# Token halves of 272 and 256 columns, and streamed tiles at multiples of 64 bytes, in a two-block fp32 network

## The chip, the cores and the metric

The kernel runs on one NeuronCore of a Trainium2 chip. The metric is the device time of one execution in microseconds (us); the times below are medians of several. The engines are PE (TensorE; PEld is its load of a stationary tile), DVE (VectorE), ACT (ScalarE), POOL (GpSimd) and SP (SyncE, which issues most DMAs here).

## The reference, cut to what matters

Two networks run one after the other on 512 tokens of width 1,024, all in float32.

```python
def reference(x, c, ctx, ...):
    x = first_block(x, c, ctx, ...)     # "block 1"
    return second_block(x, meta, ...)   # "block 2"

def second_block(x, meta_tokens, ...):
    h = jnp.concatenate([meta, x], axis=1)          # 16 + 512 = 528 tokens
    for i in range(2):
        a = rmsnorm(h, norm_mix_pre[i])
        m = forgetting_attention(a, ...) if i % 2 == 0 else gated_deltanet(a, ...)
        h = h + rmsnorm(m, norm_mix_post[i])
        f = conv_ffn(rmsnorm(h, norm_ffn_pre[i]), ...)
        h = h + rmsnorm(f, norm_ffn_post[i])
    return h[:, 16:]

def conv_ffn(h, w_up, conv_w, w_down):              # 1024 -> 2 * 2816 -> 1024
    gate, up = jnp.split(causal_dwconv(h @ w_up, conv_w), [2816], axis=-1)
    return (jax.nn.gelu(gate, approximate=True) * up) @ w_down
```

Block 1 is a layer with neighbourhood attention, a state-space scan and a feed-forward part (1,024 to 2 x 2,816 and back) on 512 tokens, with 256 context tokens beside them in the first projections. Most of the work of both blocks is dense projections of the form tokens x weight matrix.

## The kernel before

Everything on the chip lies transposed: features on the 128 partitions, tokens along the free dimension. A weight matrix is worked off in panels of 128 output columns. `panels` is the list of all of them in order, each with its stage ("q", "k", "v", "dt", "xbc", "z", "wo", "up1", "down1" in block 1; "gate", "pair", "sig", "ao", "up2", "down2", "rate", "qkv", "og", "do", "up3", "down3" in block 2), the rows it contracts (kc tiles of 128, mostly 8) and its `spans`, the stretches of tokens. Block 1's spans are 512 columns (`ONE`), or 512 and 256 (`TWO`, with the context). Block 2's are `HALF`: its 528 tokens do not fit in one PSUM bank of 512, so they are worked in two stretches, each in a bank of its own.

The products are made in three parts for the precision: a weight panel is cut into a high part `wh` (ACT, line 613) and the rest `wl` (POOL or DVE, line 623), and an activation into a high part and a rest. `tensor_mm` issues, for each panel j and each contraction tile k, high x high, rest x high and high x rest. This is line 645 of the profile, where each matmul has its own load of the stationary weight tile:

```python
wt, a = ((wh, high), (wh, low), (wl, high))[n]
for i, (t0, tn) in enumerate(p.spans):
    ins = pe.matmul(ps[bank_of(j, i)][:, 0:tn], wt[slot][:, k, :], a[:, k, t0:t0 + tn], start=first, stop=last)
```

All these operands are float32r. The moving operands (`high`, `low`) are `t_hh`/`t_hl` in the first projections of both blocks, `t_mh`/`t_ml` before w_out of block 1, `t_fhh`/`t_fhl` and `t_fh`/`t_fl` in block 1's feed-forward part, and in block 2 `t_hh`, `t_hl`, `t_oh`, `t_ol`, `t_ffh`, `t_ffl`, `t_fhh`, `t_fhl`. The profile leaves out the buffer numbers, so that `t_hh` and `t_fhh` stand for tiles of both blocks; the number of columns (512 and 256, or 264) tells them apart. A panel in block 2 is 8 x 3 x 2 = 48 matmuls. There are two slots of `wh` and `wl`: the cut of panel j waits until panel j-2 has been multiplied.

In the up stages of block 2 (88 panels, in pairs of one gate and one value panel, in groups of 8, 8 and 6 pairs for each feed-forward part), DVE takes a panel out of PSUM (line 2562), ACT starts the convolution over tokens (2736), DVE adds two more taps (2829, 2832), ACT makes the gelu (2740), DVE multiplies gate and value (2838), and ACT and POOL cut the result into high part and rest (2745, 2871). Each engine takes its work in the order in which the program lists it; semaphores join them.

Addresses: `sbt` allots the tiles of a stack one behind the other, and each starts at the next multiple of 32 bytes. A row of 528 columns is 2,112 bytes, which is 33 times 64; rows of 512 and 768 are also multiples of 64. So the base of a tile decides for all its rows. Worked out from the sizes: in the kernel before, block 1's `t_hh`, `t_hl`, `t_mh`, `t_ml` and all weight tiles start at a multiple of 64; `t_fhh`, `t_fhl`, `t_fh`, `t_fl`, and all streamed operand tiles of block 2, start at 32 modulo 64. A second half that begins at column 264 begins 1,056 bytes on, 32 modulo 64 from the base, so at a multiple of 64.

Of the kernel before, what the change touches and what calls it, by code (L numbers as in the profile page):

```python
# [19 lines left out]
L = S + NM  # L20
# [4 lines left out]
TILES = [(0, NM)] + [(NM + 128 * i, 128) for i in range(4)]  # L25
HALF = [(0, L // 2), (L // 2, L // 2)]
NEG = -1e30
# [93 lines left out]
def program(nc, io):  # L121
    ctx = ExitStack()
    with ctx:
# [43 lines left out]
        small = sbt(ctx, "small", [128, 48])  # L167
        eps = sbt(ctx, "eps", [128, 1])
        warm = sbt(ctx, "warm", [128, 1])
        part = [sbt(ctx, f"part{i}", [128, 128]) for i in range(3)]  # L170
        ssq = sbt(ctx, "ssq", [128, 6])
        roots = [sbt(ctx, f"roots{i}", [128, 20]) for i in range(4)]
# [3 lines left out]
        rstd = sbt(ctx, "rstd", [128, S + CT + 4])  # L176
        sqb = [sbt(ctx, f"sqb{i}", [128, S + CT + 4]) for i in range(2)]

        def C(name, p=128, w=128):
# [481 lines left out]
        zs = sbt(s1, "zs", [128, 4, S])  # L661
        xbc = sbt(s1, "xbc", [128, 8, NW])
        dts = sbt(s1, "dts", [128, 6, 16])
        qT = sbt(s1, "qT", [128, 4, S])
# [1201 lines left out]
        pT = [sbt(sb_, f"apt{i}", [128, 1360]) for i in range(2)]  # L1866
        inv = sbt(sb_, "ainv", [128, L // 2])
        glog = sbt(sb_, "aglog", [128, L])
# [157 lines left out]
        ASPLIT = [(0, 0, 16), (1, 0, 144), (2, 0, 272), (3, 0, 400), (4, 0, 400), (4, 400, 128)]  # L2026
        BSPLIT = [(0, 0, 264), (0, 264, 264), (1, 128, 400), (2, 256, 272), (3, 384, 144), (4, 512, 16)]
        SIGNALS.update({
# [536 lines left out]
        def forget_vector(dv, w, st):  # L2565
# [84 lines left out]
            def mixing(p, half):  # L2650
                bo, bs_ = bank("mixing", p, half)
                q0, wide = HALF[half]
                w.wait_ge(s.weighed, at("weighed", "mixing", p, half))
                if p + half:
                    w.wait_ge(s.scaled, at("scaled", "mixing", p - 1 + half, 1 - half))
                dv.reciprocal(inv[:, :], ps[bs_][:, 0:wide]).then_inc(up("inverted", "mixing", p, half), 1)
                w.wait_ge(s.inverted, at("inverted", "mixing", p, half))
                dv.tensor_tensor(acc0[:, p, q0:q0 + wide], ps[bo][:, 0:wide], inv[:, :],
                                 MUL).then_inc(up("scaled", "mixing", p, half), 1)
# [1036 lines left out]
```

## Time and profile before

| what | value |
|---|---|
| median of 3 runs | 2,736.95 us (2,735.82 to 2,739.54) |
| span of the profiled execution | 2,732.2 us |
| matmuls recorded | 19,794, one weight load each |
| TensorE busy | 2,546.3 us, 93% of the span |
| DVE, ACT, POOL busy | 1,369.3, 973.2, 985.7 us |
| read from and written to HBM | 73 GB/s over the span |

The profile is of one execution, and its span runs from its first to its last instruction. No time of that execution beside its span was given; the span is 4.7 us below the median of the runs. "Busy" of an engine is the union of its instructions' durations; matmuls overlap each other, so a steady stretch shows TensorE 100% busy whatever its pace, and the pace is read from the starts. A fp32 matmul (not float32r) is recorded as two.

### The profile page before, as it was taken

The page shows a single profiled execution, that of the slowest core. Times are in us where ns is not written, and L with a number is a line of the kernel's source. Part 1 is how long each engine was busy: PE and PEld are TensorE (multiplying, and loading weights), DVE is VectorE, ACT ScalarE, POOL GpSimd, SP SyncE. Part 2 cuts the span into 40 slices and gives each one's busy share as a digit, 9 for nine tenths or more (in the row PEclk, how much of TensorE's full clock was granted, in tenths as well). Part 3 has the DMA queues.
Part 4 walks back from the last instruction along what each step waited for, and adds up shares of the span by engine and source line. Part 5 has one row for each costly group of instructions (what it writes and reads, how often), then busy time and mean ns, then how long its engine had stood idle before and what let it go on. Part 6 is the DMA issues. An engine that isn't in the chain of part 4 may idle for free.

```text
span 2732.2 us, 45723 instructions
## 1 busy us (share of the span) xinstructions
PE 2546.3 (93%) x19794; PEld 2286.5 (84%) x19794; DVE 1369.3 (50%) x2057; ACT 973.2 (36%) x1565; POOL 985.7 (36%) x585
## 2 busy tenths in 40 slices
PE   7989978799999999999999999989998979999997
PEld 5877767678888888887999999988988968999997
DVE  4634455462635354444264554466654534727363
ACT  5234344232323444334433332354332224333232
POOL 1743344544444322222434444500002214445444
PEclk9999999999999999999999999999999988999998
DMA  9432120333332221111222332322111012233221
GB/s 248 121 94 63 53 70 24 92 96 97 93 93 87 68 55 47 40 47 40 78 62 85 89 90 85 87 59 70 40 33 36 17 32 59 85 92 87 87 87 60
DMA packets 379927, 201.33 MB, mean 74 GB/s; under 512 B 6464, under 2 KB 377152, under 8 KB 379728
## 3 DMA queue, kind: packets, MB, share of 16 engines
q1 hardware_dynamic: 379728, 198.42, 25.8%
q8 instruction: 156, 2.56, 0.4%
q14 instruction: 43, 0.35, 0.0%
HBM read 196.30 MB, written 2.10 MB: 73 GB/s over the span
## 4 chain that ended last, share of the span: by engine, by line
PE 57%; DVE 22%; ACT 11%; issue 4%; POOL 4%; DMA 1%; POOLq 0%; ACTq 0%; SPq 0%; DVEq 0%
PE ps L645 40%; DVE t_ffy L2829 7%; ACT t_wh L613 5%; DVE t_ffy L2832 2%; ACT t_ffy L2736 2%; DVE t_atq L2628 2%; POOL t_wl L623 1%; PE ps L2436 1%; DVE t_wl L623 1%; DVE t_ffy L2838 1%; PE ps L3061 1%; PE ps L2409 1%; PE ps L2375 1%; PE ps L3080 1%; PE ps L1090 1%
## 5 line engine op out<-in xcount | busy, mean ns | idle before, releaser
L623 POOL TENSOR_TENSOR t_wl<-t_raw,t_wh 128x1024 fp32r<-128x1024 f32 (+2 forms) x268 | 611.1, 2281 | 1030.1 <-ACT t_wh L613 1030.1
L613 ACT ACTIVATE t_wh<-t_raw 128x1024 fp32r<-128x1024 f32 (+2 forms) x323 | 327.7, 1015 | 605.8 <-PE ps L645 562.4
L645 PE MATMUL ps<-t_hh,t_wh 128*128 128x264 f32 (+2 forms) x2048 | 473.4, 310 | 14.4 <-DVE t_dcq L2562 3.6
L645 PE MATMUL ps<-t_hh,t_wl 128*128 128x264 f32 (+2 forms) x2048 | 449.4, 298 | 8.0 <-POOL t_wl L623 4.3
L645 PE MATMUL ps<-t_hl,t_wh 128*128 128x264 f32 (+2 forms) x2048 | 446.0, 299 | 0.0
L645 PEld LDWEIGHTS ps<-t_hh,t_wh 128*128 128x128 f32 x2048 | 323.7, 192 | 36.5 <-issue 17.6
L645 PEld LDWEIGHTS ps<-t_hh,t_wl 128*128 128x128 f32 x2048 | 324.0, 191 | 24.2 <-POOL t_wl L623 6.9
L645 PEld LDWEIGHTS ps<-t_hl,t_wh 128*128 128x128 f32 x2048 | 322.6, 191 | 9.1 <-issue 1.5
L645 PE MATMUL ps<-t_fhh,t_wh 128*128 128x264 f32 (+1 forms) x1040 | 280.9, 324 | 6.5 <-DVE t_fhl L1753 4.9
L645 PE MATMUL ps<-t_fhh,t_wl 128*128 128x264 f32 (+1 forms) x1040 | 281.5, 325 | 4.6 <-POOL t_wl L623 4.5
L2829 DVE SCALAR_TENSOR_TENSOR t_ffy<-t_ffp,t_vec,t_ffy 128x528 f32<-128x528 f32 x88 | 216.8, 2463 | 130.6 <-ACT t_ffy L2736 130.6
L645 PE MATMUL ps<-t_fhl,t_wh 128*128 128x264 f32 (+1 forms) x1040 | 278.4, 323 | 0.0
L645 PEld LDWEIGHTS ps<-t_fhh,t_wh 128*128 128x128 f32 x1040 | 173.9, 190 | 25.3 <-DVE t_fhl L1753 7.9
L645 PEld LDWEIGHTS ps<-t_fhh,t_wl 128*128 128x128 f32 x1040 | 174.2, 190 | 21.3 <-POOL t_wl L623 5.9
L645 PEld LDWEIGHTS ps<-t_fhl,t_wh 128*128 128x128 f32 x1040 | 173.5, 189 | 17.3 <-issue 0.4
L645 PE MATMUL ps<-t_ffh,t_wl 128*128 128x264 f32 x704 | 144.7, 287 | 8.6 <-POOL t_wl L623 7.8
L645 PE MATMUL ps<-t_ffh,t_wh 128*128 128x264 f32 x704 | 144.7, 287 | 5.2 <-ACT t_wh L613 1.5
L645 PE MATMUL ps<-t_ffl,t_wh 128*128 128x264 f32 x704 | 143.5, 286 | 0.0
L2562 DVE TENSOR_TENSOR t_ffp<-ps,t_rstd 128x264 f32<-128x264 f32 x176 | 67.5, 426 | 112.6 <-PE ps L645 111.6
L645 PEld LDWEIGHTS ps<-t_ffh,t_wl 128*128 128x128 f32 x704 | 109.7, 190 | 11.9 <-POOL t_wl L623 11.9
L623 DVE TENSOR_TENSOR t_wl<-t_raw,t_wh 128x1024 fp32r<-128x1024 f32 x55 | 79.0, 1437 | 79.8 <-ACT t_wh L613 79.8
L645 PEld LDWEIGHTS ps<-t_ffh,t_wh 128*128 128x128 f32 x704 | 109.3, 190 | 6.9 <-ACT t_wh L613 5.0
(558 smaller groups left out, 4351.3 us busy)
## 6 DMA issues: line engine op xcount, KB each, us to landing
t_raw<-in_up SPq DMA_DIRECT2D x44, 512.0 KB, 3.8
t_raw<-in_up2a SPq DMA_DIRECT2D x44, 512.0 KB, 3.9
t_raw<-in_up2b SPq DMA_DIRECT2D x44, 512.0 KB, 3.9
t_raw<-in_attn_in SPq DMA_DIRECT2D x33, 512.0 KB, 4.1
t_raw<-in_dn_in SPq DMA_DIRECT2D x33, 512.0 KB, 4.1
t_raw<-in_ada_w SPq DMA_DIRECT2D x32, 512.0 KB, 4.4
t_raw<-in_w_in SPq DMA_DIRECT2D x25, 512.0 KB, 4.4
t_raw<-in_down SPq DMA_DIRECT2D x16, 512.0 KB, 3.8
```

What stands on the lines that cost most here:

```text
L613: ac.activation(wh[slot_of[j]][:, 0:kc, :], raw[r % NRAW][:, 0:kc, :], ACT.Copy).then_inc(up("wh_cut", "cut", j), 1)
L623: eng.tensor_tensor(wl[slot_of[j]][:, 0:kc, :], raw[r % NRAW][:, 0:kc, :], wh[slot_of[j]][:, 0:kc, :].bitcast(F), SUB).then_inc(up(name, " ...
L645: ins = pe.matmul(ps[bank_of(j, i)][:, 0:tn], wt[slot][:, k, :], a[:, k, t0:t0 + tn], start=first, stop=last)
L1090: ins = pe.matmul(ps[b][:, 0:64], pts[i % 2][:, 128 * k:128 * k + 128], V[:, v, 64 * h:64 * h + 64], start=k == 0, stop=k == 3)
L2375: pe.matmul(ps[b][0:tn, 0:wide], aq[p % 3][64 * e:64 * e + 64, t0:t0 + tn], ak[p % 3][64 * e:64 * e + 64, a:a + wide], start=True, stop=False)
L2409: pe.matmul(ps[b][0:tn, 0:wide], ak[p % 3][64 * e:64 * e + 64, t0:t0 + tn], aq[p % 3][64 * e:64 * e + 64, q0:q0 + wide], start=True, stop= ...
L2436: ins = pe.matmul(ps[b][64 * e:64 * e + 64, lo - q0:lo - q0 + n], lhs, pT[e][0:tn, P_AT[k] + lo - t0:P_AT[k] + lo - t0 + n], start=k == 0, ...
L2562: ins = dv.tensor_tensor(a[part_, t0:t0 + tn], ap[part_, :], rstd[part_, t0:t0 + tn], MUL)
L2628: dv.reciprocal(tq[m][:, :], tq[m][:, :]).then_inc(up("inverted", "pair_norm", p, m), 1)
L2736: ac.activation(y, fp[par][:, 0:L], ACT.Copy, scale=col(f"f{n}c0", f + NF * par)).then_inc(up("copied", kind, n, f), 1)
L2829: dv.scalar_tensor_tensor(out=y, in0=u[:, 1:1 + L], scalar=col(f"f{n}c1", f + NF * par), in1=y, op0=MUL, op1=ADD).then_inc(st.up(), 1)
L2832: dv.scalar_tensor_tensor(out=y, in0=u[:, 2:2 + L], scalar=col(f"f{n}c2", f + NF * par), in1=y, op0=MUL, op1=ADD).then_inc(up("conved", ki ...
```

## The change

`HALF` becomes 272 and 256 columns instead of 264 twice. All places that use it follow: the two matmuls of each tile and part in every panel of block 2, the two instructions that take a panel out of PSUM, the sums over features, and in the attention the split of the weights' first key tile (`BSPLIT`) and of the mixing. The buffer `inv` grows to 272 columns. Three tiles of 1, 1 and 6 columns (`eps`, `warm`, `ssq`) become one of 8 (`few`), so 32 bytes in place of three times 32, and two pads of 32 bytes (`gap0`, `gap1`) are set behind the tiles that stay for the whole program and behind `xbc`.

```diff
-HALF = [(0, L // 2), (L // 2, L // 2)]
+HALF = [(0, 272), (272, 256)]
...
-        eps = sbt(ctx, "eps", [128, 1])
-        warm = sbt(ctx, "warm", [128, 1])
+        few = sbt(ctx, "few", [128, 8])
+        eps, warm, ssq = few[:, 0:1], few[:, 1:2], few[:, 2:8]
         part = [sbt(ctx, f"part{i}", [128, 128]) for i in range(3)]
-        ssq = sbt(ctx, "ssq", [128, 6])
...
         sqb = [sbt(ctx, f"sqb{i}", [128, S + CT + 4]) for i in range(2)]
+        sbt(ctx, "gap0", [128, 8])
...
         xbc = sbt(s1, "xbc", [128, 8, NW])
+        sbt(s1, "gap1", [128, 8])
...
-        inv = sbt(sb_, "ainv", [128, L // 2])
+        inv = sbt(sb_, "ainv", [128, HALF[0][1]])
...
-        BSPLIT = [(0, 0, 264), (0, 264, 264), (1, 128, 400), (2, 256, 272), (3, 384, 144), (4, 512, 16)]
+        BSPLIT = [(0, 0, 272), (0, 272, 256), (1, 128, 400), (2, 256, 272), (3, 384, 144), (4, 512, 16)]
...
-                dv.reciprocal(inv[:, :], ps[bs_][:, 0:wide]).then_inc(up("inverted", "mixing", p, half), 1)
+                dv.reciprocal(inv[:, 0:wide], ps[bs_][:, 0:wide]).then_inc(up("inverted", "mixing", p, half), 1)
```

What it does to the addresses, again worked out from the sizes: `t_fhh`, `t_fhl`, `t_fh`, `t_fl` and the streamed operand tiles of block 2's panels go from 32 to 0 modulo 64, and both halves of block 2 begin at a multiple of 64. Nothing moves for block 1's `t_hh`, `t_hl`, `t_mh`, `t_ml` and the weight tiles. Tiles behind an odd number of 32-byte tiles go the other way: `t_aq`, `t_ak`, `t_av`, `t_atq` and `t_ablk` of the attention from 0 to 32.

The program has 16,867 matmuls before and after, in the same order. TensorE's instructions in the attention, where a piece of the panels meets the mixing product of the first half (line 2436, stationary `t_av` or ones, moving `t_apt`). Before:

```order
L645 MATMUL ps<-t_hl,t_wh 128x264 x2
L645 MATMUL ps<-t_hh,t_wl 128x264 x2
L2436 MATMUL ps<-t_apt,t_av 64x264 x2
L2436 MATMUL ps<-t_apt,t_cst 64x264 x2
L2436 MATMUL ps<-t_apt,t_av 64x136 x2
L2436 MATMUL ps<-t_apt,t_cst 64x136 x2
L2436 MATMUL ps<-t_apt,t_av 64x8 x2
L2436 MATMUL ps<-t_apt,t_cst 64x8 x2
```

And the same place after (the line is 2437 then):

```order
L645 MATMUL ps<-t_hl,t_wh 128x272
L645 MATMUL ps<-t_hl,t_wh 128x256
L645 MATMUL ps<-t_hh,t_wl 128x272
L645 MATMUL ps<-t_hh,t_wl 128x256
L2437 MATMUL ps<-t_apt,t_av 64x272 x2
L2437 MATMUL ps<-t_apt,t_cst 64x272 x2
L2437 MATMUL ps<-t_apt,t_av 64x144 x2
L2437 MATMUL ps<-t_apt,t_cst 64x144 x2
L2437 MATMUL ps<-t_apt,t_av 64x16 x2
L2437 MATMUL ps<-t_apt,t_cst 64x16 x2
```

Nothing changed its place; only the widths did, and what the mixing of the first half gains (8 columns a tile) the second half loses.

DVE's instructions at the same mixing product and the panel taken out beside it (`t_ainv` is the reciprocal of the weights' sum, `t_acc` the mixed values, `t_aq` a panel of queries). Before:

```order
L2642 TENSOR_REDUCE t_amx<-ps 128x1 x10
L2647 TENSOR_TENSOR t_amx<-t_amx 128x2
L2656 RECIPROCAL t_ainv<-ps 128x264
L2658 TENSOR_TENSOR t_acc<-ps,t_ainv 128x264
L2562 TENSOR_TENSOR t_aq<-ps,t_rstd 128x264 x2
```

And after:

```order
L2643 TENSOR_REDUCE t_amx<-ps 128x1 x10
L2648 TENSOR_TENSOR t_amx<-t_amx 128x2
L2657 RECIPROCAL t_ainv<-ps 128x272
L2659 TENSOR_TENSOR t_acc<-ps,t_ainv 128x272
L2563 TENSOR_TENSOR t_aq<-ps,t_rstd 128x272
L2563 TENSOR_TENSOR t_aq<-ps,t_rstd 128x256
```

Again the order is the same, and one instruction has 8 columns more and its partner 8 fewer.

## Rows read from the trace of the kernel before

**Rows 1.** The page: span, busy time by engine.

```profile
span 2732.2 us, 45723 instructions
...
PE 2546.3 (93%) x19794; PEld 2286.5 (84%) x19794; DVE 1369.3 (50%) x2057; ACT 973.2 (36%) x1565; POOL 985.7 (36%) x585
```

**Rows 2.** The chain that ended last, the whole span, by line.

```profile
PE ps L645 40%; DVE t_ffy L2829 7%; ACT t_wh L613 5%; DVE t_ffy L2832 2%; ACT t_ffy L2736 2%; DVE t_atq L2628 2%; POOL t_wl L623 1%; PE ps L2436 1%; DVE t_wl L623 1%; DVE t_ffy L2838 1%; PE ps L3061 1%; PE ps L2409 1%; PE ps L2375 1%; PE ps L3080 1%; PE ps L1090 1%
```

**Rows 3.** The same chain in 515:912, by line.

```profile
by line: PE ps L645 89.1%; DVE t_sqb L1749 1.5%; issue 1.5%; ACT t_fhh L1583 1.5%; POOL t_wl L623 1.2%; DVE t_rstd L553 0.9%; PE ps L489 0.7%; PE ps L476 0.7%; DVE t_gy L1765 0.6%; ACT t_wh L613 0.5%; DVE t_xT L2794 0.5%; PE ps L498 0.4%; P
```

**Rows 4.** The chain in 912:1358, 1358:1800, 1800:2290 and 2290:2732, in this order.

```profile
by line: PE ps L645 36.5%; DVE t_atq L2628 10.1%; PE ps L2436 8.0%; PE ps L2409 5.7%; PE ps L2375 5.4%; DVE t_ainv L2656 3.6%; issue 3.1%; PE ps L2385 2.6%; PE ps L2416 2.6%; ACT t_atq L2496 2.0%; PE ps L2350 2.0%; ACT L2496 1.8%; PE ps L23
...
by line: PE ps L645 38.2%; DVE t_ffy L2829 22.5%; ACT t_wh L613 10.0%; DVE t_ffy L2832 7.1%; ACT t_ffy L2736 5.8%; issue 5.6%; DVE t_ffy L2838 3.3%; POOL t_wl L623 2.6%; PE ps L2772 0.9%; PE ps L476 0.7%; PE ps L489 0.6%; ACT t_hh L2722 0.3
...
by line: PE ps L645 29.8%; PE ps L3061 5.5%; PE ps L3080 4.6%; issue 4.3%; PE ps L3084 3.8%; DVE t_wl L623 3.2%; ACT t_wh L613 3.1%; DVE t_dv L3330 2.9%; PE ps L3016 2.3%; DVE t_dq L3330 2.1%; PE ps L3147 2.0%; DVE t_dk L3330 1.8%; POOL t_w
...
by line: PE ps L645 33.8%; DVE t_ffy L2829 22.4%; ACT t_wh L613 10.0%; DVE t_ffy L2832 7.1%; issue 5.9%; ACT t_ffy L2736 5.8%; DVE t_ffy L2838 3.3%; POOL t_wl L623 2.6%; PE ps L489 1.0%; PE ps L498 1.0%; DVE t_xT L2803 0.9%; PE ps L2784 0.8
```

**Rows 5.** Groups by line and form, engine PE: count | busy us, mean ns | idle.

```profile
L645 PE MATMUL ps<-t_hh,t_wh 128*128 128x264 f32 x1712 | 371.0, 298 | 12.1 <-DVE t_dcq L2562 3.6 <-ACT t_hh L2722 3.5 <-ACT t_wh L613 2.6
...
L645 PE MATMUL ps<-t_ffh,t_wh 128*128 128x264 f32 x704 | 144.7, 287 | 5.2 <-ACT t_wh L613 1.5 <-POOL t_ffl L2871 1.5 <-ACT t_acc L2543 1.1
...
L645 PE MATMUL ps<-t_fhh,t_wh 128*128 128x264 f32 x688 | 141.9, 287 | 1.6 <-DVE t_ffp L2562 1.6
...
L645 PE MATMUL ps<-t_fhh,t_wh 128*128 128x512 f32 x352 | 139.0, 395 | 4.9 <-DVE t_fhl L1753 4.9
...
L645 PE MATMUL ps<-t_fh,t_wh 128*128 128x512 f32 x176 | 69.4, 394 | 0.0
...
L645 PE MATMUL ps<-t_oh,t_wh 128*128 128x264 f32 x256 | 54.3, 293 | 3.6 <-POOL t_ol L3518 2.4 <-POOL t_ol L2693 1.2
```

**Rows 6.** Timeline, PE, block 1's up stage: start us, us, what.

```profile
699.63 0.40 PE L645 MATMUL ps<-t_fhh,t_wl 128*128 128x512 f32 x1
...
702.43 0.40 PE L645 MATMUL ps<-t_fhh,t_wl 128*128 128x512 f32 x1
```

**Rows 7.** Timeline, PE, a panel of w_out in block 1.

```profile
471.00 0.39 PE L645 MATMUL ps<-t_mh,t_wh 128*128 128x512 f32 x1
...
476.22 0.39 PE L645 MATMUL ps<-t_mh,t_wl 128*128 128x512 f32 x1
```

**Rows 8.** Timeline, PE, a block 1 panel of 512 and 256 columns.

```profile
83.45 0.52 PE L645 MATMUL ps<-t_hl,t_wh 128*128 128x512 f32 x2
...
91.08 0.51 PE L645 MATMUL ps<-t_hh,t_wl 128*128 128x512 f32 x2
```

**Rows 9.** The same view inside that panel, one pair.

```profile
86.11 0.28 PE L645 MATMUL ps<-t_hh,t_wl 128*128 128x256 f32 x1
86.23 0.39 PE L645 MATMUL ps<-t_hh,t_wh 128*128 128x512 f32 x1
```

**Rows 10.** Timeline, PE, a block 2 panel, two halves of 264.

```profile
1546.43 0.42 PE L645 MATMUL ps<-t_hh,t_wh 128*128 128x264 f32 x2
...
1552.27 0.42 PE L645 MATMUL ps<-t_hh,t_wh 128*128 128x264 f32 x2
```

**Rows 11.** By stretch, groups 0 and 1 of block 2's first up: PE, PEld, DVE, ACT, POOL.

```profile
1399.50:1459.00 59.50, 59.05 (x477) 57.98 (x477) 42.92 (x46) 22.21 (x30) 29.78 (x16) 1.00 0.31 89
1517.20:1604.60 87.40, 87.40 (x720) 87.35 (x719) 58.68 (x61) 32.31 (x44) 43.40 (x21) 1.00 0.31 90
```

**Rows 12.** Timeline, DVE, two pairs of up panels.

```profile
1542.92 2.38 DVE L2829 SCALAR_TENSOR_TENSOR t_ffy<-t_ffp,t_vec,t_ffy 128x528 f32<-128x528 f32 x1 [1.36 <-ACT t_ffy L2736]
...
1554.95 2.38 DVE L2829 SCALAR_TENSOR_TENSOR t_ffy<-t_ffp,t_vec,t_ffy 128x528 f32<-128x528 f32 x1 [1.61 <-ACT t_ffy L2736]
```

**Rows 13.** The chain in order of time, same stretch: start us, us, what.

```profile
1541.22 1.05 ACT t_wh L613
```

**Rows 14.** Timeline, POOL, same stretch.

```profile
1542.34 2.39 POOL L623 TENSOR_TENSOR t_wl<-t_raw,t_wh 128x1024 fp32r<-128x1024 f32 x1 [3.08 <-ACT t_wh L613]
```

More of the change, by code:

```diff
@@ L2655, in mixing @@
                     w.wait_ge(s.scaled, at("scaled", "mixing", p - 1 + half, 1 - half))
-                dv.reciprocal(inv[:, :], ps[bs_][:, 0:wide]).then_inc(up("inverted", "mixing", p, half), 1)
+                dv.reciprocal(inv[:, 0:wide], ps[bs_][:, 0:wide]).then_inc(up("inverted", "mixing", p, half), 1)
                 w.wait_ge(s.inverted, at("inverted", "mixing", p, half))
-                dv.tensor_tensor(acc0[:, p, q0:q0 + wide], ps[bo][:, 0:wide], inv[:, :],
+                dv.tensor_tensor(acc0[:, p, q0:q0 + wide], ps[bo][:, 0:wide], inv[:, 0:wide],
                                  MUL).then_inc(up("scaled", "mixing", p, half), 1)
```

## The prediction

> **What bounds the kernel now.** I read the page first: of a span of 2,732.2 us TensorE is busy 2,546.3 (93%), and no other engine reaches 51% [rows 1]. That looks as if every ns taken off a matmul came back. The chain that ended last says otherwise: the streamed products of line 645 are 40% of it, and DVE, ACT and POOL stand between them [rows 2]. So I split the chain at the stages. In 515:912, block 1's feed-forward, line 645 is 89.1% [rows 3]. In block 2 it is 36.5, 38.2, 29.8 and 33.8% of four stretches of 446, 442, 490 and 442 us [rows 4]. That is 162.8 + 168.8 + 146.0 + 149.5 = 627 us, of 1,820.
>
> Then I read the pace of the streamed products from start to start in steady stretches, since the busy time of one holds latency that the next one covers (the page has 395 ns for one of 512 columns). The clock is at its upper level there, 1.00 or 2.4 GHz [rows 11], so 512 columns stream in 213.3 ns. Four cases, with the address of the moving operand, modulo 64, from the section on the kernel:
> - 512 columns from a base at 32: 2.80 us for 12, 233.3 ns each [rows 6];
> - 512 columns from a base at 0: 5.22 us for 23, 227.0 each [rows 7];
> - 512 and 256 columns in turn, both from 0: 7.63 us for 22 pairs, 346.8 a pair [rows 8], of which the narrow one is about 117 (0.12 by the two rows) and the wide one 230 [rows 9];
> - 264 twice, from 32 and from 0: 5.84 us for 24 pairs, 243.3 a pair [rows 10].
>
> The first two have the same columns, one matmul for each weight tile, and differ in the base. 6.4 ns is the time in which 2.4 GHz streams 15 columns, and 64 bytes are 16 columns: as if a stretch of 64 bytes that is touched in part cost a whole one. 512 columns from 32 touch 33 stretches, from 0 they touch 32; 227.0 / 32 = 7.09 ns for each.
>
> **The change, part by part.**
>
> *Block 1's operands at a multiple of 64.* t_fhh, t_fhl, t_fh and t_fl move from 32 to 0. They are read by (352 + 176) x 3 = 1,584 matmuls of 512 columns [rows 5]. On the chain are 89.1% of 397 = 353.7 us, or 353.7 / 0.2333 = 1,516 of them [rows 3]. At 6.4 ns each: **9.7 us**. The bounds are nothing (the base is not the reason) and 1,584 x 6.4 = 10.1. I take 9.7, because nothing else separates rows 6 from rows 7.
>
> *Block 2's pair.* Lengths 264 + 264 touch 17 + 17 stretches: the first starts at 32 and ends on a boundary, the second starts on it and ends inside one. 272 + 256 touch 17 + 16. The number of columns is 528 in both. By the price of a stretch the pair is 34 x 7.09 = 241.1 now, and 2.2 less than measured; the 512 and 256 pair is 48 x 7.09 = 340.3, and 6.5 less than measured. So a new pair costs 33 x 7.09 = 234.0 and 2.2 to 6.5 more: 236.2 to 240.5. From the other side, if the excess over pure streaming (346.8 - 320.0 = 26.8) is one for each pair of aligned matmuls and 64 bytes play no part, the new pair is 220.0 + 26.8 = 246.8, 3.5 more than now. I take 239.3, in the upper half of the first interval since it is nearest the pair that also alternates wide and narrow: **4.0 ns less** a pair. Ends: 7.1 less, 3.5 more.
>
> How many pairs pay? All four groups of 264 in rows 5 times 3 make 10,080 matmuls, 5,040 pairs. But 627 us of chain are 627 / 0.2433 = 2,577 pairs. The rest hides behind other work, and the up stages show what. Their panels come in pairs, gate and value. TensorE needs 2 x 5.84 = 11.68 us for two [rows 10]; DVE's line 2829 comes back after 1,554.95 - 1,542.92 = 12.03 [rows 12]. That loop holds no matmul: ACT cuts the weights (1.05) [rows 13], POOL makes the low part (2.39, from 1,542.34 to 1,544.73) [rows 14], DVE's line 2829 takes 2.38 and ends 0.6 after POOL [rows 12], although it reads no more than its neighbours, and ACT takes the next cut only after what DVE feeds it. In group 0 TensorE already keeps the loop's pace, 59.5 us for 477 matmuls or 124.7 each; in group 1 it runs ahead at 87.4 / 720 = 121.4 [rows 11] and waits at the end. A faster pair there only makes that wait longer, and up to 12.03 - 11.68 = 0.35 us per two panels a slower one costs nothing.
>
> 2,577 x 4.0 = 10.3 us. In the attention and the delta rule the chain changes engine every few us, and what runs beside it is close behind; I take a fifth off: **8.2 us**.
>
> *The rest.* DVE's and ACT's evacuations go from 264 + 264 to 272 + 256 columns, the same sum. The mixing products of line 2436 keep their number and their sum of columns; fp32 streams at half the pace, so that a stretch has double the time to arrive. t_aq and t_ak move from 0 to 32, and some 400 fp32 matmuls of the attention stream them; t_dT, t_dY and t_dTT move from 32 to 0, read by more, but short ones. At a full 6.4 ns the first is 2.6 us lost, and the second as much won. I take nothing for both, and keep 3 us each way. Semaphores, waits and queues stay as they are, and the three small tiles in one lie in front of everything.
>
> A page speaks against all of this. The Trainium skill, "TensorE: Matmul & The Clock Gate", section "Back-to-back issue gap", has the gap between two matmuls depend on the columns alone (columns / 2.4 + 2.5 ns), and "SBUF — State Buffer", section "Specifications (TRN2)", has lines of 16 bytes, which a base at 32 meets as well as one at 0. By the first an estimate for 512 columns is 215.8 ns; the trace does not agree, it has 227.0 and 233.3. By both pages of the Trainium skill the change would give nothing, and the sum would be 0 in place of 17.9.
>
> **Sum.** 9.7 + 8.2 = 17.9 us. On the profiled execution that is 2,732.2 - 17.9 = 2,714.3 of span; the median shown, 2,736.95, is 4.7 longer than that span, which I keep: 2,719.0.
>
> **The rivals.**
> - *The stretch is the whole story, and all of it is on the path.* The pair falls to 236.2, 2,577 x 7.1 = 18.3, with 9.7 makes 28.0: **2,709**. For it: 233.3 against 227.0. Against it: the 512 and 256 pair lies 6.5 above that rule. Chance 0.18.
> - *Block 2 gives nothing.* What the 256 wins the 272 gives back. 2,736.95 - 9.7 = **2,727.3**. For it: 528 columns are streamed either way. 0.08.
> - *Aligned pairs carry 26.8 whatever their length.* 2,577 x 3.5 = 9.0 lost against 9.7 won: **2,736**, no change. For it: the measured 346.8. Against it: the 264 pair, with 23.3, would then be better for being misaligned. 0.06.
> - *The base plays no part*, and rows 6 and 7 differ by the stage (other weights, other DMA). Then block 2's price per stretch falls too: **2,737**. Against it: both run without a wait and at one matmul per weight tile. 0.06. (The two pages of the Trainium skill named above end here too.)
> - *Slower: the weight load is laid bare.* A load runs beside each matmul, and TensorE's load row is busy 87.35 of 87.40 us [rows 11]. If a load wants the 121.7 ns that a 264 gives it, the 256 gets no shorter, and the 272 pays the 16.7 (230 - 213.3) that the wide member pays in rows 9: 121.7 + 113.3 + 16.7 = 251.7, 8.4 more. 2,577 x 8.4 = 21.6, less 9.7: **2,749**. It decides from 15.2 / 2,577 = 5.9 ns a pair. Against it: a 256 passes at 117 in rows 9, loads and all. 0.05.
>
> **How the numbers follow.** The forecast, 0.57, spans 2,713 to 2,727: a pair at 236.2 or at 242, and 3 us for the fp32 products. With the first two rivals it is 0.83, and they reach from 2,709 to 2,727.3; the range is 2,707 to 2,731, which leaves out the last three. A measurement of this kernel tells 0.2% (5.5 us) from no change. Faster: 0.57 + 0.18 + 0.08 = 0.83. Same: 0.06 + 0.06 = 0.12. Slower: 0.05.
>
> **What would show it.** In the changed kernel's timeline: 24 matmuls of t_fhh and t_fh in 5.44 us, not 5.60; a block 2 panel (24 pairs) in 5.74 us, not 5.84 (5.67 by the first rival, 5.92 by the third, 6.04 by the last); line 2829 (2830 then) still every 12.03 us, with a longer wait of TensorE at the start of the down stages; line 645's share of the chain smaller in block 1. I am wrong if the 256 stays at 121, or if DVE's loop moves with the new addresses, since I take it for fixed: 1% of it is 44 x 0.12 = 5.3 us.

## The result, and the profile after

The changed kernel took 2,741.3 us (median of 20 runs, 2,738.4 to 2,745.8), the kernel before 2,736.2 (20 runs, 2,733.8 to 2,743.3): a ratio of 1.0016, 95% interval 1.001 to 1.0022. It is 5 us slower, where 18 us faster was forecast; the prediction itself had set 0.2% (5.5 us) as the least that it would call a change. The profiled execution took 2,742.6 us, its span 2,740.1.

The page of the changed kernel, the lines that answer to [rows 1], and the row of the granted clock:

```profile
span 2740.1 us, 45723 instructions
...
PE 2554.2 (93%) x19794; PEld 2296.2 (84%) x19794; DVE 1368.6 (50%) x2057; ACT 972.8 (36%) x1565; POOL 985.3 (36%) x585
...
PEclk9999989999999999999999999999999898999998
```

TensorE is busy 8 us longer for the same instructions; nobody else is. The chain in 515:912, as in [rows 3], still belongs to the streamed products:

```profile
by line: PE ps L645 88.9%; issue 1.5%; DVE t_sqb L1750 1.5%; ACT t_fhh L1584 1.5%; POOL t_wl L623 1.2%; DVE t_rstd L553 0.9%; DVE t_gy L1766 0.6%; ACT t_wh L613 0.5%; PE ps L476 0.5%; PE ps L489 0.4%; POOL t_raw L920 0.3%; POOL t_rstd L553 
```

The timeline of TensorE in the changed kernel, at the places of [rows 6, 7, 10] (start us, us, what; 24 matmuls or 24 pairs lie between the two rows of each couple):

```profile
471.40 0.39 PE L645 MATMUL ps<-t_mh,t_wl 128*128 128x512 f32 x1
...
476.89 0.39 PE L645 MATMUL ps<-t_mh,t_wl 128*128 128x512 f32 x1
...
697.00 0.39 PE L645 MATMUL ps<-t_fhh,t_wl 128*128 128x512 f32 x1
...
702.58 0.40 PE L645 MATMUL ps<-t_fhh,t_wl 128*128 128x512 f32 x1
...
1551.33 0.40 PE L645 MATMUL ps<-t_hh,t_wl 128*128 128x272 f32 x2
...
1557.17 0.29 PE L645 MATMUL ps<-t_hh,t_wl 128*128 128x272 f32 x1
```

- t_fhh, whose base is now a multiple of 64: 5.58 us, where 5.44 was forecast and 5.60 was before. The first steady panels of the stage still take 5.60, and so do the last four; those between take 5.58.
- The block 2 panel with 272 and 256 columns: 5.84 us, as with 264 twice.
- t_mh, whose address did not move: 5.49 us, 5.44 before. Nothing in the prediction's account can make this panel slower. **This row is the loose thread.** What did move there is the other operand: merging three small tiles into one set all weight tiles 64 bytes lower, which left them at a multiple of 64 and which I therefore passed over.

The same happens in the first projections of block 1 (operand t_hh, not moved either). Rows of the changed kernel, 21 pairs of 512 and 256 columns apart:

```profile
84.40 0.51 PE L645 MATMUL ps<-t_hl,t_wh 128*128 128x512 f32 x2
...
91.80 0.52 PE L645 MATMUL ps<-t_hl,t_wh 128*128 128x512 f32 x2
```

7.40 / 21 = 352.4 ns a pair, against 346.8 in [rows 8].

Then I followed the start of the last streamed matmul at some ends of stages through the traces, of each kernel two executions (the second ones are e4 and e8 below). The last two columns give how long the granted clock stood at 0.50 in the stretch up to there:

| end of | before, twice | changed, twice | mean change in the stretch | at 0.50 before, twice | at 0.50 changed, twice |
|---|---|---|---|---|---|
| q, k, v and dt | 162.6, 162.3 | 164.1, 163.3 | +1.2 | 10.2, 10.2 | 13.7, 10.2 |
| w_out | 511.9, 515.0 | 516.5, 515.8 | +1.5 | 30.7, 37.5 | 37.5, 37.5 |
| block 1's feed-forward | 905.7, 908.8 | 909.3, 909.0 | -0.8 | 6.8, 6.8 | 6.8, 6.8 |
| attention (ao) | 1348.8, 1351.3 | 1354.7, 1354.4 | +2.6 | 6.8, 3.4 | 10.2, 10.2 |
| feed-forward (up2, down2) | 1769.0, 1771.5 | 1773.5, 1773.4 | -1.3 | 10.2, 10.2 | 6.8, 6.8 |
| delta rule (do) | 2282.9, 2285.6 | 2292.7, 2292.0 | +4.9 | 54.6, 54.6 | 64.9, 68.3 |
| feed-forward (up3, down3) | 2704.2, 2707.0 | 2712.8, 2712.9 | -0.8 | 13.7, 13.7 | 10.2, 10.2 |

Between two executions of one kernel the first 515 us differ by up to 3 us; from there to the end the difference stays within 0.7 us. As far as two executions tell, what happens behind 515 belongs to the program. Most of it sits in the attention and the delta rule, in steps of 1.5 and 3.3 us at single panels. A stretch at half clock in which TensorE sets the pace loses half its length. By that reckoning the clock makes +2.6, -1.7, +6.0 and -1.7 us of the last four stretches, where +2.6, -1.3, +4.9 and -0.8 were measured: 5.1 of 5.4 us in all. At the largest step, by stretch: busy us and number of instructions of PE, PEld, DVE, ACT, POOL, granted clock, DMA. The kernel before:

```profile
2109.70:2116.50 6.80, 6.80 (x69) 6.21 (x66) 1.86 (x4) 1.72 (x5) 0.00 (x0) 1.00 0.14 41
2116.50:2123.30 6.80, 6.80 (x62) 6.59 (x62) 3.76 (x11) 3.72 (x5) 1.41 (x1) 1.00 0.00 0
```

The changed kernel at the same instructions:

```profile
2114.40:2121.20 6.80, 6.80 (x70) 6.21 (x67) 1.85 (x4) 1.77 (x5) 0.00 (x0) 1.00 0.14 41
2121.20:2128.00 6.80, 6.80 (x36) 6.45 (x35) 1.90 (x6) 3.58 (x5) 0.00 (x0) 0.50 0.00 0
```

The work ahead is the same, TensorE is busy all the time in both, and in one of them the granted clock falls to 0.50 (1.2 GHz): 36 matmuls go through where 62 did. 6.8 us at half speed cost 3.4. It is the 3.3 us step.

The clock works the other way too. What the changed kernel wins in up2 and down2 is a fall that only the kernel before has, in both of its executions (1,484.6 in e4). The kernel before:

```profile
1481.80:1485.20 3.40, 3.40 (x18) 3.40 (x17) 0.00 (x0) 0.00 (x0) 1.54 (x1) 0.50 0.67 186
```

The changed kernel at the same instructions:

```profile
1487.70:1491.10 3.40, 3.40 (x31) 3.40 (x29) 0.00 (x0) 0.00 (x0) 1.56 (x1) 1.00 0.68 187
```

### The profile page after: what moved, and what is told of

It is laid out like the page before. It is cut to its first block, busy times and chain, and to the rows that moved or that the text cites. A ratio compares the mean times of both kernels' runs of the same rounds, so it can differ in the third digit from the quotient of the medians.

```text
span 2740.1 us, 45723 instructions
## 1 busy us (share of the span) xinstructions
PE 2554.2 (93%) x19794; PEld 2296.2 (84%) x19794; DVE 1368.6 (50%) x2057; ACT 972.8 (36%) x1565; POOL 985.3 (36%) x585
## 4 chain that ended last, share of the span: by engine, by line
PE 57%; DVE 22%; ACT 11%; issue 5%; POOL 4%; DMA 1%; POOLq 0%; ACTq 0%; SPq 0%; DVEq 0%
PE ps L645 40%; DVE t_ffy L2830 7%; ACT t_wh L613 5%; DVE t_ffy L2833 2%; ACT t_ffy L2737 2%; DVE t_atq L2629 2%; POOL t_wl L623 1%; PE ps L2437 1%; DVE t_wl L623 1%; DVE t_ffy L2839 1%; PE ps L3062 1%; PE ps L2410 1%; PE ps L2376 1%; PE ps L3081 1%; PE ps L1091 1%
## 5 line engine op out<-in xcount | busy, mean ns | idle before, releaser
L645 PE MATMUL ps<-t_hh,t_wh 128*128 128x256 f32 (+2 forms) x2048 | 474.4, 311 | 14.4 <-DVE t_dcq L2563 3.6
L645 PE MATMUL ps<-t_hh,t_wl 128*128 128x256 f32 (+2 forms) x2048 | 451.8, 300 | 8.4 <-POOL t_wl L623 5.4
L645 PE MATMUL ps<-t_hl,t_wh 128*128 128x256 f32 (+2 forms) x2048 | 447.3, 299 | 0.0
L645 PE MATMUL ps<-t_fhh,t_wh 128*128 128x512 f32 (+2 forms) x1040 | 280.8, 324 | 6.5 <-DVE t_fhl L1754 4.9
L645 PE MATMUL ps<-t_fhh,t_wl 128*128 128x512 f32 (+2 forms) x1040 | 280.6, 324 | 4.7 <-POOL t_wl L623 4.6
L645 PE MATMUL ps<-t_fhl,t_wh 128*128 128x512 f32 (+2 forms) x1040 | 278.3, 323 | 0.0
L645 PE MATMUL ps<-t_ffh,t_wl 128*128 128x272 f32 x704 | 144.9, 287 | 8.3 <-POOL t_wl L623 7.8
L645 PE MATMUL ps<-t_ffh,t_wh 128*128 128x272 f32 x704 | 143.4, 285 | 5.2 <-POOL t_ffl L2872 1.5
L645 PE MATMUL ps<-t_ffl,t_wh 128*128 128x272 f32 x704 | 142.8, 284 | 0.0
L2563 DVE TENSOR_TENSOR t_ffp<-ps,t_rstd 128x272 f32<-128x272 f32 (+1 forms) x176 | 67.5, 425 | 111.1 <-PE ps L645 110.2
```

Of the source, the lines that this page charges most:

```text
L2563: ins = dv.tensor_tensor(a[part_, t0:t0 + tn], ap[part_, :], rstd[part_, t0:t0 + tn], MUL)
```

## The experiments

Two questions came out of this. Does the pace of a streamed product hang on where its moving tile lies, or on where that lies **against the weight tile**? And do the falls of the clock belong to what the changed kernel does, or only to when it does it? "Distance" below is the address of the moving tile less that of the weight tile, modulo 256, worked out from the sizes in the order of allotment. In block 1 it is the same for every contraction tile and every weight slot, since weights advance by 512 bytes from tile to tile and 4,096 from slot to slot, and the moving tile by 2,048. In block 2 the moving tile's rows of 2,112 bytes walk by 64. Before: t_mh 0, t_fhh 96. Changed: t_mh 64, t_fhh 128. In block 2 the third weight slot (for one panel at the start of a stage) is left out. Ratios are to runs of the kernel before made beside each experiment.

### The parts of the change, alone

**e1: only the halves.** The edits to `HALF`, `BSPLIT` and `inv` of the diff, no pads.

> Only the halves become 272 and 256 (the divisor tile of the attention grows by 32 bytes with them); no pads, so the moving operands stay at 32 modulo 64 as before. If a partly touched 64-byte stretch costs 7.09 ns, 272 from 32 touches 18 and 256 from 32 touches 17, 35 in place of 34: the panel goes from 5.84 to about 6.0 us and the time to about 2,736 + 2,577 x 7.1 ns = 2,754. If only the 528 columns count, the panel stays at 5.84 and block 1 at 5.60, and the time is that of before, about 2,736, unless the split itself is what cost the 5 us of the whole change; then about 2,741.

Measured: 2,742.6 us, ratio 1.0019 (1.001 to 1.0028). Its timeline, 24 pairs of a panel apart:

```profile
1553.24 0.41 PE L645 MATMUL ps<-t_hh,t_wl 128*128 128x272 f32 x2
...
1559.11 0.41 PE L645 MATMUL ps<-t_hh,t_wl 128*128 128x272 f32 x2
```

5.87 us, not the 6.0 of the stretch rule, but not the 5.84 of before either: 1.2 ns a pair, up to 3 us over the 2,577 pairs on the chain. Block 1 stands at 5.60. The halves alone cost as much as the whole change.

**e2: only the pads.** The edits to `few`, `gap0`, `gap1`, halves of 264.

> Only the pads: streamed operands at 0 modulo 64, halves 264 and 264 as before. By the 64-byte stretch block 1 gains 9.7 us and the pair touches 17 + 17 stretches as before: about 2,726. If the base plays no part, block 1's panels stay between 5.57 and 5.60 (gain 0 to 1 us): about 2,735 if the 5 us that the whole change lost belong to the split, about 2,741 if they belong to the addresses or to where the clock falls.

Measured: 2,740.3 us, 1.0015 (1.0006 to 1.0024). t_fhh 5.60 at first and 5.58 later, t_mh 5.49, as in the changed kernel. A panel in up2 takes 5.87 here too (median), and the granted clock falls at the place of the 3.3 us step. The parts cost +5.9 and +3.6, together +5: they do not add up, which speaks against a fixed price for either, though each has an interval of some 2.5 us to both sides.

**e3: only the weight tiles, 64 bytes lower.**

```diff
+        few = sbt(ctx, "few", [128, 8])        # in place of eps, warm, ssq
...
         sqb = [sbt(ctx, f"sqb{i}", [128, S + CT + 4]) for i in range(2)]
+        sbt(ctx, "gap0", [128, 16])
```

> The kernel before with the raw, high and low weight tiles alone 64 bytes lower (as the changed kernel has them); every moving operand where it was. If the distance of weight and moving tile sets the pace, the panel of t_mh goes from 5.44 to 5.49 and that of t_fhh changes from 5.60 too. If neither address plays a part, both stay (5.44 and 5.60) or move by chance from one execution to the next, and the time is 2,736 within 2 us.

Measured: 2,740.7 us, 1.0015 (1.0006 to 1.0024). No moving tile has moved, and t_mh takes 5.49; t_fhh, at distance 160 now:

```profile
700.65 0.40 PE L645 MATMUL ps<-t_fhh,t_wl 128*128 128x512 f32 x1
...
706.27 0.40 PE L645 MATMUL ps<-t_fhh,t_wl 128*128 128x512 f32 x1
```

5.62 us. The weight tile's place is part of the pace. This is also the only edit of the change that was not meant to do anything, and it costs 4 us.

**e4 and e8: the two kernels again, unchanged.**

> The kernel before, unchanged, for a second profiled execution. Theory of the clock: the dips of the granted clock (about 1.5 us each in the difference of the two traces) lie at other places from one execution to the next; the ratio is 1.000 within 0.001. Rival: they are fixed by the program, and the two traces of this kernel lie on one another within 0.5 us at each panel; then the changed kernel's 5 us are its own. The panels of t_mh at 5.44 and t_fhh at 5.60 repeat if the program sets them.

> The changed kernel, unchanged, for a second profiled execution. If its falls of the clock in the delta rule belong to it, the granted clock is again below 0.7 in 2,120 to 2,130 and the span again loses some 3 us there against the kernel before; if they come and go by execution, this trace lacks one of them. The t_fhh panel repeats 5.60 first and 5.57 later if the program sets it.

Measured: 2,737.5 us, 1.0004 (0.9995 to 1.0013), and 2,741.7 (one run). The panels repeat: t_mh 5.44, t_fhh 5.60 in e4; 5.60 and then 5.58 in e8. Of the falls, e4 has those of the kernel before in block 2, but for 3.4 us near 942. e8 repeats the steps of 1.5 us at 1,019 and 2,271, but its 3.3 us lie earlier, in two falls that are 3.4 us longer than in the changed kernel's first execution: one below, and one at 2,090 (0.50 over 6.8 us, where the changed kernel has 0.75). The changed kernel in 2,054.8:2,074.8, and e8 at the same instructions:

```profile
2054.80:2074.80 20.00, 15.87 (x122) 15.07 (x120) 11.60 (x21) 7.25 (x13) 4.07 (x2) 0.83 0.11 27
```

```profile
2055.00:2075.00 20.00, 15.88 (x110) 15.08 (x109) 10.84 (x18) 5.92 (x9) 4.06 (x2) 0.74 0.11 27
```

0.83 against 0.74, and at 2,123.8 the clock is 1.00 in e8. Both lose the same by the end. The rival "fixed by the program" is right in the sum, and the place can shift by a wait or two from one execution to the next.

### The distance

**e5: one pad of 32 bytes behind the weights.** t_fhh at distance 128, t_mh at 32.

```diff
+        sbt(ctx, "gap0", [128, 8])             # behind sqb; nothing else changed
```

> The kernel before with one pad of 32 bytes between the weight tiles and the streamed tiles: t_fhh and the tiles of block 2 at 0 modulo 64 (64 modulo 128), t_mh and t_ml at 32 modulo 64, weights where they were (64 modulo 128). By the 64-byte stretch the t_fhh panel falls from 5.60 to 5.44 and the t_mh panel rises from 5.44 to 5.60. If the place of the weight tiles sets the pace and the base of the moving tile only a little, t_mh stays within 0.02 of 5.44 and t_fhh within 0.03 of 5.60. Time 2,726 by the first; 2,736 to 2,741 by the second.

Measured: 2,739.4 us, 1.0011 (1.0001 to 1.002). t_fhh 5.58, t_mh 5.60. Neither side was right: the stretch rule for t_mh, the other for t_fhh. With t_mh at a base of 32 this run alone can't tell base from distance; the next can.

**e6: weight tiles at 32 modulo 64, streamed tiles at 0.** `few` and `gap1` as in the change, and 32 bytes of pad ahead of `raw`. t_mh at a base of 0 and distance 32; t_fhh at a base of 0 and distance 96, as it was in the kernel before.

> Streamed tiles at 0 modulo 64 as in the changed kernel, halves of 264, and the weight tiles at 32 modulo 64. If what matters is that the weight tile, not the moving one, lies across a boundary of 64 bytes, the panels are the slowest of all: t_mh above 5.49, t_fhh above 5.62. If the weight tile's place plays no part, t_mh 5.44 and t_fhh 5.57 to 5.60. One look, so the time tells only a loss above 5 us.

Measured: 2,734.9 us (one run). Its timeline:

```profile
466.56 0.40 PE L645 MATMUL ps<-t_mh,t_wl 128*128 128x512 f32 x1
...
472.16 0.40 PE L645 MATMUL ps<-t_mh,t_wl 128*128 128x512 f32 x1
...
700.60 0.40 PE L645 MATMUL ps<-t_fhh,t_wl 128*128 128x512 f32 x1
...
706.20 0.40 PE L645 MATMUL ps<-t_fhh,t_wl 128*128 128x512 f32 x1
```

t_mh, at the very address it has in the kernel before, takes 5.60 and not 5.44. And t_fhh, aligned, keeps the 5.60 it had unaligned at the same distance. Each of the two expectations has one panel right and the other wrong.

**e7: streamed tiles at 0, weights at 64 modulo 128.** As e6, without the pad ahead of `raw`, with two of the four `roots` and `gap0` behind `sqb`: t_fhh at distance 320 = 64, t_mh at 256 = 0.

> Streamed tiles at 0 modulo 64 as in the changed kernel, halves of 264, but the weight tiles at 64 modulo 128 as in the kernel before (two of the small root tiles lie behind them instead of ahead). If the weights at 64 modulo 128 give the 227 ns and the aligned moving tile is needed with it, t_fhh falls to 5.44 and the time to about 2,727 to 2,730. If only the weights' place matters and little, t_mh returns to 5.44, t_fhh stays 5.57 to 5.60, and the time is 2,736 to 2,739, better than pads alone (2,740). If neither, t_mh stays at 5.49 and the time at 2,740.

Measured: 2,733.2 us, 0.999 (0.9981 to 1.0).

```profile
467.29 0.39 PE L646 MATMUL ps<-t_mh,t_wl 128*128 128x512 f32 x1
...
472.73 0.39 PE L646 MATMUL ps<-t_mh,t_wl 128*128 128x512 f32 x1
...
700.26 0.39 PE L646 MATMUL ps<-t_fhh,t_wl 128*128 128x512 f32 x1
...
705.75 0.39 PE L646 MATMUL ps<-t_fhh,t_wl 128*128 128x512 f32 x1
```

5.44 and 5.49. Of the two expectations for t_fhh (5.44, and 5.57 to 5.60) neither came; 5.49 is what t_mh takes at distance 64. From here the distance modulo 256 fits every panel of block 1, and e9, e14 and e16 were forecast with it.

**e9: distance 0 for both, bases at 32.**

```diff
+        rstd = sbt(ctx, "rstd", [128, S + CT + 4])      # ahead of raw, not behind wl
+        sqb = [sbt(ctx, f"sqb{i}", [128, S + CT + 4]) for i in range(2)]
         raw = [sbt(ctx, f"raw{i}", [128, KD, 128]) for i in range(NRAW)]
...
         xbc = sbt(s1, "xbc", [128, 8, NW])
+        sbt(s1, "gap1", [128, 24])
...
+        sbt(s2, "gap2", [128, 24])
         ssum = sbt(s2, "ssum", [128, L])
```

(and `few` in place of the three small tiles).

> The kernel before with rstd and sqb ahead of the weight tiles and 96 bytes of pad ahead of block 1's t_mh and ahead of block 2's tiles, so that the distance from weight tile to moving tile is a multiple of 256 bytes for t_fhh as for t_mh, while both moving tiles start at 32 modulo 64; block 2's distances are those of before. Theory of the distance (the nine traces so far agree with: 5.44 us a panel at 0 modulo 256, 5.49 at 64, 5.58 to 5.60 at 128, 5.60 at 32 and 96, 5.62 at 160): both panels 5.44, 10 us less, about 2,726 and falls of the clock on top, 0 to 8 us. By the 64-byte stretch: both 5.60, so about 2,737.

Measured: 2,729.4 us, 0.9973 (0.9963 to 0.9984).

```profile
466.12 0.39 PE L644 MATMUL ps<-t_mh,t_wl 128*128 128x512 f32 x1
...
471.56 0.39 PE L644 MATMUL ps<-t_mh,t_wl 128*128 128x512 f32 x1
...
697.29 0.39 PE L644 MATMUL ps<-t_fhh,t_wl 128*128 128x512 f32 x1
...
702.73 0.39 PE L644 MATMUL ps<-t_fhh,t_wl 128*128 128x512 f32 x1
```

5.44 both. That is the 6.4 ns a matmul (6.7 by whole panels) which the prediction gave to block 1, here with every moving tile of block 1 at 32 modulo 64. It is 7.3 us faster than the kernel before; 10.6 were to be had (66 panels of 0.16).

**e14: rstd alone ahead of the weights.** No streamed tile moves; t_fhh at distance 64, t_mh at 224.

> The kernel before with the tile rstd ahead of the weights in place of behind them; no streamed tile moves. The distance modulo 256 of t_fhh becomes 64 (from 96), that of t_mh 224 (from 0). Theory of the distance: the t_fhh panel 5.49 (as at 64 and 320 so far), 7 us less in block 1; t_mh slower than 5.44, and if the pace is even about 0 near the 5.60 of 32. By the 64-byte stretch nothing changes: 5.60 and 5.44, about 2,737.

Measured: 2,734.5 us, 0.9983 (0.9973 to 0.9993).

```profile
469.90 0.40 PE L645 MATMUL ps<-t_mh,t_wl 128*128 128x512 f32 x1
...
475.50 0.40 PE L645 MATMUL ps<-t_mh,t_wl 128*128 128x512 f32 x1
...
701.35 0.39 PE L645 MATMUL ps<-t_fhh,t_wl 128*128 128x512 f32 x1
...
706.85 0.39 PE L645 MATMUL ps<-t_fhh,t_wl 128*128 128x512 f32 x1
```

5.50 by the rows (5.493 over many panels) and 5.60: both as forecast.

All panels of 24 matmuls of 512 columns, by distance:

| distance mod 256 | us | where |
|---|---|---|
| 0 | 5.44 | t_mh before, e4, e7, e9; t_fhh e9 |
| 64 | 5.49 | t_mh changed, e3; t_fhh e7, e14 |
| 128 | 5.58 to 5.60 | t_fhh changed, e2, e5, e8 |
| 32, 224 | 5.60 | t_mh e5, e6, e14 |
| 96 | 5.60 | t_fhh before, e1, e4, e6 |
| 160 | 5.62 | t_fhh e3 |

Bases at 0 and at 32 modulo 64 stand side by side in the rows of 0, 64, of 32 and 224, and of 96, with one pace each. That 256 and not 512 is the measure rests on t_mh (256) and t_fhh (320) in e7.

**e12, e13, e16: block 2.** On e9. In up3 the operand's rows become 576 columns, so that the distance no longer walks:

```diff
+        sbt(s1, "gap3", [128, 24])             # e16: 56
-        fhh1 = sbt(s1, "fhh1", [128, KD, L], R)
-        fhl1 = sbt(s1, "fhl1", [128, KD, L], R)
+        fhh1 = sbt(s1, "fhh1", [128, KD, 576], R)[:, :, 0:L]
+        fhl1 = sbt(s1, "fhl1", [128, KD, 576], R)[:, :, 0:L]
```

e12 has halves of 264 at distance 0 and 32, e13 halves of 256 and 272 both at 0, e16 halves of 264 at 128 and 160.

> On top of e9: the two operand tiles of up3 (t_fhh, t_fhl of block 2's second feed-forward) get rows of 576 columns, 2,304 bytes, in place of 528, and 96 bytes of pad, so that the first half lies at distance 0 modulo 256 from the first two weight slots for every k and the second half (264 columns on) at 32; before, the distance walked by 64 bytes from k to k. If block 2's pairs follow the distance as block 1's matmuls do, the panels of up3 change from 5.84 by 0.05 or more, and differ from slot to slot (the third weight slot lies at 128). If the pair has a floor of its own, every panel of up3 stays at 5.84 to 5.88 and the time is that of e9, 2,729, within 3 us.

> As e12, with halves of 256 and 272 columns all through block 2, so that in up3 both halves lie at distance 0 modulo 256 from the first two weight slots. If the pairs follow the distance, this is their best case and up3's panels fall below 5.80; if the pair has a floor of its own, 5.84 to 5.87 as with all other halves so far.

> e12 with 128 more bytes of pad ahead of up3's operand tiles: rows of 576 columns as there, but the first half at 128 modulo 256 from the first two weight slots and the second at 160, the worst distances of block 1. If the distance is what made e12's panels 5.76, they are 5.84 or more here; if it was the longer row, they stay at 5.76.

Measured: 2,728.6 us, 0.9961 (0.9948 to 0.9975); 2,727.0, 0.9957 (0.9944 to 0.9971); 2,728.6, 0.9969 (0.9956 to 0.9982). A panel of up3 in e12, and one in e16:

```profile
2333.90 0.41 PE L644 MATMUL ps<-t_fhh,t_wh 128*128 128x264 f32 x2
...
2339.66 0.28 PE L644 MATMUL ps<-t_fhh,t_wh 128*128 128x264 f32 x1
```

```profile
2480.08 0.41 PE L644 MATMUL ps<-t_fhh,t_wh 128*128 128x264 f32 x2
...
2486.00 0.41 PE L644 MATMUL ps<-t_fhh,t_wh 128*128 128x264 f32 x2
```

5.76 and 5.92 with the same rows of 576: the distance moves block 2's pairs too, by 6.7 ns a pair from best to worst. With rows of 528 it walks through near and far, which a panel of 5.84, the middle, fits. The expected difference by weight slot can't be read: the third slot serves one panel, beside the waits at the start of the stage. Elsewhere block 2 does not follow so plainly: over up2 the median panel is 5.84 in the kernel before, the changed one, e3, e4, e6, e9, e12 and e16, 5.86 in e13 and 5.87 in e1, e2, e5, e7, e14 and e15, and the changed kernel's up3 has 5.84 in one execution and 5.88 in the other. What decides between them is open. In e13 a panel takes 5.85, so even halves beat uneven ones at the best distance; why is open too. And the time barely moves: panels of e12's up3 come as 5.76 and, where the loop of DVE, ACT and POOL is the pace, 6.24, together 12.0 us for two, the 12.03 of [rows 12].

### The clock

**e10 and e11: a little more work in block 1.** The kernel before with the first matmul of four panels issued twice (0.93 us), and the changed kernel with that of twelve (2.8 us).

```diff
+                    if first and 84 <= j < 88:          # e11: 84 <= j < 96
+                        pe.matmul(ps[bank_of(j, i)][:, 0:tn], wt[slot][:, k, :], a[:, k, t0:t0 + tn], start=True,
+                                  stop=True)
                     ins = pe.matmul(...)
```

> The kernel before, in which the first matmul of panels 84 to 87 (block 1's feed-forward, TensorE the bound) is issued twice: 0.93 us of added work, all else the same. Theory of the clock (a delay of less than a microsecond decides whether a wait of TensorE in block 2 is followed by half clock): the trace shows falls in 2,120 to 2,130 or at the delta rule's second wait that before did not have, and the time is 3 to 6 us longer. Rival (the falls belong to the changed program's own waits): 0.9 us longer, about 2,737.5.

> The changed kernel with the first matmul of panels 84 to 95 issued twice: 2.8 us of added work. Theory of the clock: block 2 stands against the falls at about the place where it stood in the kernel before, some of the added falls (1,026, 2,125, 2,279) are gone, and the time stays at or below that of the changed kernel, 2,738 to 2,741, although it does more. Rival: 2.8 us longer, 2,744.

Measured: 2,739.5 us, 1.0011 (1.0002 to 1.002), and 2,742.8, 1.0022 (1.0013 to 1.0031). In e10, at the instructions of the two stretches shown above:

```profile
2111.30:2118.10 6.80, 6.80 (x70) 6.21 (x67) 1.85 (x4) 1.78 (x5) 0.00 (x0) 1.00 0.14 41
2118.10:2124.90 6.80, 6.80 (x36) 6.45 (x34) 1.90 (x6) 3.54 (x5) 0.00 (x0) 0.50 0.00 0
```

The kernel before, delayed by less than a microsecond some 1,300 us earlier, shows the changed kernel's fall at this place. It is one execution, and two things weaken it. The changed kernel's own second execution, e8, lacks the fall here, so that the place moves without any edit. And e4 runs 2.5 to 3.1 us behind the first execution of the kernel before all through block 2, three times the added work, and has that kernel's falls. The last streamed matmul of e10 starts 5.7 us later than in the first execution of before and 2.9 later than in e4. By the medians it lost 2.7, of which 0.9 are the added work; the 1.8 left are less than expected, and with some 2.5 us of interval to both sides not clear of nothing. (The places in the expectation of e11, 1,026, 2,125 and 2,279, are misread; the falls meant stand at 1,019, 2,121 and 2,271.) e11 is 1.4 above the changed kernel for 2.8 of work; its fall at 1,019 is gone, that at 2,122 is not. Its interval overlaps that of the changed kernel, so this decides nothing.

**e15: the halves of the change on e9's layout.**

> e9 with the halves of the change, 272 and 256. If the halves cost by themselves (evacuations, pairs), it is 4 to 6 us above e9, as the halves alone were above the kernel before. If what they cost there was where the clock's falls landed, it is within 3 us of e9 or below it, and the trace shows the falls of block 2 at other panels than e9's.

Measured: 2,730.7 us, 0.9973 (0.9963 to 0.9983), the ratio of e9 itself. On the old layout the same halves cost 5.9 us. So they have no fixed price of that size; the 5.87 us a panel is there on both layouts. Its trace has the fall that stands at 2,121 in the changed kernel, at 2,112, which e9's lacks, and its last streamed matmul starts 8.8 us behind e9's: single executions of these two kernels differ by more than their medians.

## Why the prediction was wrong

- **"I take 9.7, because nothing else separates rows 6 from rows 7" is the step that failed.** They were separated by the address of the moving tile modulo 64, and as well by its distance from the weight tile, 96 against 0 modulo 256, for which I had no column. The price, 6.4 ns a matmul, was real; e9 earned it with moving tiles at 32 modulo 64, and e6 lost it with t_mh at 0. In the changed kernel the distance went from 96 to 128, which is worth 5.60 to 5.58: some 1 us of the 9.7 (the stretch is 0.8 shorter).
- **The pair, "4.0 ns less", so 8.2 us, failed with it.** Measured 0 in the rows shown: 243.3 before and after (245 in up3 of e8). The price per stretch of 64 bytes came from the same two groups and fell with them. The rival "block 2 gives nothing" had this part right, and "the base plays no part" had both parts; but its reason, that the stage makes the difference, was wrong: e3 and e6 change the pace of one stage by moving the weights. It gave 2,737, the nearest of all, and a chance of 0.06.
- **That nothing moves for t_hh, t_mh and the weight tiles**, in the section on the change, held modulo 64 only. They went 64 bytes lower, and t_hh and t_mh from distance 0 to 64. The first projections pay 5.6 ns for each of 408 pairs, 2.3 us at most:

```profile
L645 PE MATMUL ps<-t_hl,t_wh 128*128 128x256 f32 x136 | 38.7, 284 | 0.0
```

  (136 for each of the three products). 216 of these pairs lie ahead of 162.6, for which the traces have +1.2; the panels of t_mh add some 0.4. But the clock stood at 0.50 for longer too in these first 515 us, so that the traces alone don't part the two there.
- **The rest, "I take nothing for both, and keep 3 us each way", lacked the clock.** The prediction let the granted clock be the same in both kernels. In both executions of each, the loss behind 912 lies where the clock falls in one kernel and not in the other: +2.6 in the attention and +4.9 in the delta rule, against -1.3 and -0.8 in block 2's feed-forward parts, where it is the kernel before that has the more. The slower rival, a weight load laid bare in the 256, did not occur: its panel takes 5.84.
- What the prediction took for fixed was: line 2829 (2830 now) has a median of 2,386 ns, 2,384 before.
- The Trainium skill, "TensorE: Matmul & The Clock Gate", section "Back-to-back issue gap", gives the gap from the columns alone (columns / 2.4 + 2.5 ns) as the gap of an isolated matmul, and says that in a stream the load counts too; addresses it does not name. The runs show that they count: with 512 columns it goes from 226.7 to 234.3 ns with nothing but addresses changed.

How much of the 5 us in the medians is distance and how much is clock is not settled. Distance accounts for at most some 2 us net (2.3 + 0.4 - 0.8). That the falls make the rest is what the traces show of two executions of each kernel; no run took all of them out of the changed kernel and left the rest. The mean granted clock of all runs is 0.9692 for the changed kernel (20 runs) and 0.9697 for the kernel before (32 runs, beside e1 to e4), which is 1.5 us over the span, less than its scatter. Why a fall comes in one kernel and not in the other isn't shown either. And e3 did without them: it has none of the added falls of the delta rule, behind 912 it takes 1,798.1 us as e4 does (1,798.2), and its 4 us can be all distance (1.5 at 160, at most 2.3 and 0.4 at 64). What in the chip makes the distance count isn't shown by any run; a row of the weight tile is 512 bytes, and 128, the farthest from 0 modulo 256, is not the worst.

## What to carry to other kernels

When two stretches differ in pace, list everything that differs between them, the address of the other operand included, before one of it is given the price; then ask the trace for a panel that the theory says can't change. An edit that "moves nothing" moves the addresses of all that lies behind it, and here a reorder of three tiles with some pads (e9) was worth more than the whole planned change was in the other direction. In this kernel small edits came with falls of the clock in other places, worth up to 5 us in a stage: for gains of 0.2% compare two traces of each kernel, and add up the time at half clock stage by stage before looking for another cause.

## What was not expected of the hardware

- Back-to-back float32r matmuls of 512 columns take 226.7, 228.9, 232 to 233, 233.3 or 234.3 ns, by the distance of moving and weight tile modulo 256 bytes (0; 64; 128; 32, 96 and 224; 160). Pairs of 264 take 240.0 ns at distances 0 and 32 and 246.7 at 128 and 160.
- At distance 128 the pace changed between 5.60 and 5.58 us a panel in the middle of a stage, at different panels in the changed kernel (after some 16 of the feed-forward's, and back for the last four) and e8 (after some 40), with nothing changed in the program.
- Behind the same instructions, with TensorE busy throughout, the granted clock stood at 1.00 in one kernel and at 0.50 in another (2,116.5 before, 2,121.2 changed, 2,118.1 in e10). Behind block 1's feed-forward, time at 0.50 accounts for 5.1 of the 5.4 us between the kernels' traces.
- Best times: 2,727.0 us (e13) and 2,728.6 (e12), 0.43% and 0.39% below the kernel before.
